# Gated product at byte 128 modulo 512 of a partition, and the last down projection in pieces of 4 contraction tiles by 512 columns

## What is computed

```python
def conv_ffn(h, w_up, conv_w, conv_b, w_down):
    u = causal_dwconv(h @ w_up, conv_w, conv_b)
    g, val = u[..., :D_FF], u[..., D_FF:]
    return (jax.nn.gelu(g, approximate=True) * val) @ w_down
...
        h = rms_norm(x, norm_ffn_pre[layer])
        f = conv_ffn(h, ffn_w_up[layer], ffn_conv_w[layer], ffn_conv_b[layer], ffn_w_down[layer])
        x = x + rms_norm(f, norm_ffn_post[layer])
```

## Time and profile before

| what | before |
|---|---|
| median of 3 runs | 1133.59 us (1133.54 to 1134.7) |
| the profiled execution's own time | 1133.48 us |
| its span in the profile | 1131.6 us |
| PE busy | 1114.8 us, 99% |
| granted clock of TensorE, mean | 0.999 |
| layer 0, down projection | about 472 to 599 us |
| layer 1, down projection with its tail | about 998 us to the end |

### The profile page before, as it was taken

The page is one execution under the profiler, slowest core; times in us unless marked ns, Lnnn a source line. Parts: engine busy times, 40 slices in busy tenths (PEclk is TensorE's granted clock), DMA queues, the critical chain, the costliest instruction groups (busy, mean ns, idle before and its releaser), DMA issues.

```text
span 1131.6 us, 16487 instructions
## 1 busy us (share of the span) xinstructions
PE 1114.8 (99%) x6564; PEld 963.5 (85%) x6564; DVE 682.2 (60%) x901; ACT 502.1 (44%) x715; POOL 68.4 (6%) x56
## 2 busy tenths in 40 slices
PE   8999999999999999999999999999999999999998
PEld 7877778998888888888899877898788888899998
DVE  5674477587776676722248677478877667652222
ACT  5556766544444343421225456554534434442221
POOL 3000000230000000001003000023000000000000
PEclk9999999999999999999999999999999999999999
DMA  7311211413243332232212624231423324222232
GB/s 222 113 59 55 66 47 61 126 42 109 76 110 98 87 111 77 99 103 93 84 66 76 181 73 152 64 86 39 111 82 103 108 78 111 86 92 96 73 103 76
DMA packets 147629, 104.50 MB, mean 92 GB/s; under 512 B 4658, under 2 KB 144626, under 8 KB 147570
## 3 DMA queue, kind: packets, MB, share of 16 engines
q1 hardware_dynamic: 147538, 103.66, 30.6%
q10 hardware_dynamic: 32, 0.01, 0.0%
HBM read 98.02 MB, written 2.10 MB: 88 GB/s over the span
## 4 chain that ended last, share of the span: by engine, by line
PE 82%; DVE 9%; issue 3%; ACT 3%; DMA 2%; SPq 1%; DVEq 0%; ACTq 0%
PE ps L1529 25%; PE ps L1531 25%; PE ps L1530 25%; PE ps L1750 2%; SPq L523 1%; DVE hx_lo L1315 1%; DVE w_lo L1025 1%; DVE ps L1305 1%; DVE x L1311 1%; PE ps L1734 1%; PE ps L1763 1%; DVE cv L1361 1%; DVE cg L1361 1%; ACT prob L980 1%; PE ps L1605 1%
## 5 line engine op out<-in xcount | busy, mean ns | idle before, releaser
L1529 PE MATMUL ps<-hx_hi,w_hi 128*128 128x512 f32 (+1 forms) x944 | 360.6, 382 | 4.4 <-DVE w_lo L1057 1.9
L1530 PE MATMUL ps<-hx_lo,w_hi 128*128 128x512 f32 (+1 forms) x944 | 354.0, 375 | 0.0
L1531 PE MATMUL ps<-hx_hi,w_lo 128*128 128x512 f32 (+1 forms) x944 | 354.0, 375 | 0.0
L1025 DVE TENSOR_TENSOR w_lo<-w_raw,w_hi 128x2048 fp32r<-128x2048 f32 (+1 forms) x87 | 194.9, 2241 | 153.8 <-ACT w_hi L647 153.7
L647 ACT ACTIVATE w_hi<-w_raw 128x2048 fp32r<-128x2048 f32 (+1 forms) x87 | 162.6, 1869 | 141.9 <-DMA w_raw<-in_ffn_w_down 112.9
L1529 PEld LDWEIGHTS ps<-hx_hi,w_hi 128*128 128x128 f32 x944 | 177.6, 188 | 40.0 <-issue 4.6
L1531 PEld LDWEIGHTS ps<-hx_hi,w_lo 128*128 128x128 f32 x944 | 177.6, 188 | 32.2
L1530 PEld LDWEIGHTS ps<-hx_lo,w_hi 128*128 128x128 f32 x944 | 177.7, 188 | 31.8 <-issue 1.7
L1529 PE MATMUL ps<-w_hi,g_hi 128*128 128x256 f32 x352 | 99.0, 281 | 0.0
L887 ACT ACTIVATE cg<-ug,vec 128x512 f32<-128x512 f32 x44 | 35.9, 816 | 141.5 <-DVE ug L1352 141.5
L1531 PE MATMUL ps<-w_hi,g_lo 128*128 128x256 f32 x352 | 98.6, 280 | 0.0
(11 more groups left out here) (238 smaller groups left out, 1669.0 us busy)
## 6 DMA issues: line engine op xcount, KB each, us to landing
w_raw<-in_ffn_w_up SPq DMA_DIRECT2D x84, 512.0 KB, 4.6
w_raw<-in_ffn_w_down SPq DMA_DIRECT2D x16, 1024.0 KB, 5.0
w_raw<-in_even_w_in SPq DMA_DIRECT2D x8, 1024.0 KB, 5.1
w_raw<-in_ffn_w_down SPq DMA_DIRECT2D x8, 768.0 KB, 4.3
w_raw<-in_odd_w_qkv SPq DMA_DIRECT2D x6, 1024.0 KB, 5.1
w_raw<-in_even_w_out SPq DMA_DIRECT2D x4, 1024.0 KB, 4.9
w_raw<-in_odd_w_o SPq DMA_DIRECT2D x3, 1024.0 KB, 5.3
rsw<-rp SPq DMA_DIRECT2D x40, 64.0 KB, 2.0
```

Source lines behind the costliest of these rows:

```text
L1025: dve.tensor_tensor(w_lo[s][:, 0:k], w_raw[s][:, 0:k], w_hi[s][:, 0:k], ALU.subtract).then_inc(w_lo_done, 1)
L1529: pe.matmul(dst, s_hi, r_hi, start=first, stop=False)
L1530: pe.matmul(dst, s_hi, r_lo, start=False, stop=False)
L1531: return pe.matmul(dst, s_lo, r_hi, start=False, stop=last)
```

## The change

It does four things. The gated product begins at the next byte that is 128 modulo 512 (160 bytes further on). The mixers' buffers begin 320 bytes behind it, at 448 modulo 512. Layer 1's down projection is cut into two halves of 512 columns with pieces of 4 contraction tiles (`WIDE_K`: five of 4 and one of 2), again 12 units; a slot of 8 tiles by 256 columns is read as 4 tiles by 512 columns. Each token tile of a half has a PSUM bank of its own, and the last two pieces of the second half run token tile by token tile. The tail has two column groups in place of four. The arithmetic per output is the same, with sums over the contraction in the same order of tiles.

```diff
+WIDE_K = [(0, 4), (4, 8), (8, 12), (12, 16), (16, 20), (20, FT)]
+WIDE_TAIL = 4
...
+    def begin_at(r):
+
+        where[0] += (r - where[0]) % 512
...
-    big0 = where[0]
+    begin_at(128)
+    g0 = where[0]
+    big0 = g0 + 320
 
     g_hi = place("g_hi", [P, FT, T], F32R)
     g_lo = place("g_lo", [P, FT, T], F32R)
+    where[0] += big0 - g0
...
+    def wide(w):
+
+        return w[:].rearrange("p (k a) b n -> p k (a b n)", a=2)
+
+    def wide_bank(half, t):
+
+        g = group_of(U_DOWN[1])
+        if half == 0:
+            return bank((group_banks(g), group_banks(g) + 1, 6, 7)[t])
+        return bank((group_banks(g + 2), group_banks(g + 2) + 1, turn_bank(0), turn_bank(1))[t])
...
+            if layer == 1:
+                for half in range(2):
+                    for c, (k0, k1) in enumerate(WIDE_K):
+                        u = U_DOWN[1] + len(WIDE_K) * half + c
+                        slot_free(u)
+                        src = w_down[k0 * P:k1 * P, T * half:T * half + T].rearrange("(k p) n -> p k n", p=P)
+                        load(u, src, wide(w_raw[slot(u)])[:, 0:k1 - k0])
+                continue
...
+        def token_squares(half, t):
+
+            if half == 0 and t == TT - 1:
+                act.wait_ge(unit_done, U_DOWN[1] + len(WIDE_K))
             else:
+                act.wait_ge(mtok_mm, (TT - 1) * half + t + 1)
+            if TT * half + t >= 2:
+                act.wait_ge(mtok_sq, TT * half + t - 1)
+            act.activation(sq[t % 2][:], wide_bank(half, t), ACT.Square, accum_out=narrow[:, t, half:half + 1]).then_inc(mtok_sq, 1)
...
+        def token_gains(half, t):
...
+            dve.wait_ge(mtok_sq, TT * half + t + 1)
+            if half == 1:
+                dve.tensor_tensor(narrow[:, t, 4:5], narrow[:, t, 0:1], narrow[:, t, 1:2], ALU.add).then_inc(tok_sum, 1)
+            cols = slice(T * half, T * half + T)
+            dve.tensor_tensor(m_tok[:, t, cols], wide_bank(half, t), last_gain[:, cols], ALU.mult).then_inc(mtok_done, 1)
...
+        def wide_part(half, t, c):
+
+            u = U_DOWN[1] + len(WIDE_K) * half + c
+            k0, k1 = WIDE_K[c]
+            r_hi, r_lo = wide(w_hi[slot(u)]), wide(w_lo[slot(u)])
             for k in range(k0, k1):
+                last = three(wide_bank(half, t), g_hi[:, k, P * t:P * t + P], g_lo[:, k, P * t:P * t + P],
+                             r_hi[:, k - k0], r_lo[:, k - k0], k == 0, k == FT - 1)
...
+            banks_free(g_end)
+            for c in range(n):
+                unit_ready(U_DOWN[1] + c)
+                pe.wait_ge(g_ready, FT + WIDE_K[c][1])
+                for t in range(TT):
+                    last = wide_part(0, t, c)
...
+                if c < 4:
+                    if c == 0:
+                        banks_free(g_end + 1)
+                    turn_x(c)
+            banks_free(g_end + 2)
             pe.wait_ge(xtok_copied, DT)
+            for c in range(WIDE_TAIL):
+                unit_ready(U_DOWN[1] + n + c)
+                for t in range(TT):
+                    last = wide_part(1, t, c)
+                last.then_inc(unit_done, 1)
+            for c in range(WIDE_TAIL, n):
+                unit_ready(U_DOWN[1] + n + c)
             for t in range(TT):
+                for c in range(WIDE_TAIL, n):
+                    last = wide_part(1, t, c)
+                last.then_inc(mtok_mm, 1)
```

More of the change, by code:

```diff
@@ L899, in ffn_up @@
             act.activation(tile_(g_hi, j), cv[:], ACT.Copy).then_inc(g_hi_done, 1)
[L901 to L906, removed]
-            else:
[L908 to L911, removed]
@@ new lines, in last_down @@
+        def last_down():
+            n = len(WIDE_K)
+            for half in range(2):
+                for c in range(n):
+                    v = U_DOWN[1] + n * half + c + 2
+                    if v < N_UNITS:
+                        k0, k1 = WIDE_K[(c + 2) % n]
+                        split_hi(v, 2 * (k1 - k0))
+                    if half == 1 and c == n - 1:
+                        act.preload_act_table_set("sqrt_and_others")
+                    if half == 0 and c < 4:
+                        for i in (2 * c, 2 * c + 1):
+                            act.wait_ge(xtok_mm, i + 1)
+                            act.activation(x_tok[:, :, P * i:P * i + P], bank(turn_bank(i)).rearrange("p (t c) -> p t c", c=P),
+                                           ACT.Copy).then_inc(xtok_copied, 1)
+                for t in range(TT):
+                    token_squares(half, t)
+                    if half == 1:
+                        act.wait_ge(tok_sum, t + 1)
+                        act.activation(std[:, t:t + 1], narrow[:, t, 4:5], ACT.Sqrt, scale=1.0 / D, bias=eps).then_inc(tok_std, 1)
@@ L930, in ffn @@
                 ffn_up(layer, j, U_UP[layer] + j)
+            if layer == 1:
+                last_down()
+                return
             for mp in range(4):
                 for c in range(3):
-                    u = U_DOWN[layer] + 3 * mp + c
+                    u = U_DOWN[0] + 3 * mp + c
                     v = u + 2
-                    if v < U_DOWN[layer] + N_DOWN:
+                    if v < U_DOWN[0] + N_DOWN:
                         k0, k1 = DOWN_K[(3 * mp + c + 2) % 3]
                         split_hi(v, k1 - k0)
[L938 to L943, removed]
-                    if c == 2 and mp < 3:
[L945 to L954, removed]
+                    if c == 2 and mp < 3:
+                        whole_squares(1, mp, u)
         out_projection(0)
@@ L1389, in last_gains, with last_down @@
             dve.wait_ge(tok_rms, t + 1)
-            dve.wait_ge(mtok_done, 6 + t + 1)
+            dve.wait_ge(mtok_done, TT + t + 1)
             dve.wait_ge(xtok_copied, DT)
             for h in range(2):
-                half = slice(h * D // 2, (h + 1) * D // 2)
-                dve.scalar_tensor_tensor(out=m_tok[:, t, half], in0=m_tok[:, t, half], scalar=rcol[:, t:t + 1],
-                                         in1=x_tok[:, t, half], op0=ALU.mult, op1=ALU.add).then_inc(out_done, 1)
+                part = slice(h * D // 2, (h + 1) * D // 2)
+                dve.scalar_tensor_tensor(out=m_tok[:, t, part], in0=m_tok[:, t, part], scalar=rcol[:, t:t + 1],
+                                         in1=x_tok[:, t, part], op0=ALU.mult, op1=ALU.add).then_inc(out_done, 1)
+        def last_down():
+            n = len(WIDE_K)
+            for half in range(2):
+                for c in range(n):
+                    v = U_DOWN[1] + n * half + c + 2
+                    if v < N_UNITS:
+                        k0, k1 = WIDE_K[(c + 2) % n]
+                        split_lo(v, 2 * (k1 - k0))
+                for t in range(TT):
+                    token_gains(half, t)
         def ffn(layer):
@@ L1935, in ffn @@
                 unit(u0 + j, hx)
-            g_up = group_of(U_DOWN[layer])
+            if layer == 1:
+                return
+            g_up = group_of(U_DOWN[0])
             for mp in range(3):
@@ L1940, in ffn @@
                 for c, (k0, k1) in enumerate(DOWN_K):
-                    u = U_DOWN[layer] + 3 * mp + c
+                    u = U_DOWN[0] + 3 * mp + c
                     unit_ready(u)
[L1943 to L1970, removed]
+                    pe.wait_ge(g_ready, k1)
@@ L1971, in last_part @@
+                    columns(u, range(k1 - k0), gg, b0, k_last=FT - 1, koff=k0, signal_first=c == 2).then_inc(unit_done, 1)
+        def wide_part(half, t, c):
+            u = U_DOWN[1] + len(WIDE_K) * half + c
+            k0, k1 = WIDE_K[c]
+            r_hi, r_lo = wide(w_hi[slot(u)]), wide(w_lo[slot(u)])
             for k in range(k0, k1):
-                r = [w[slot(u)][:, k - k0].rearrange("p b n -> p (b n)") for w in (w_hi, w_lo)]
-                last = three(last_tokens(t), g_hi[:, k, P * t:P * t + P], g_lo[:, k, P * t:P * t + P], r[0], r[1], k == 0, k == FT - 1)
@@ L2120, in _ @@
         ffn(1, 2)
-        last_unit()
+        last_down()
     es.close()
```

71 lines of the change are left out of this document (28 added, 43 removed).

## The result

The changed kernel takes 1126.30 us (median of 4 runs, 1125.82 to 1126.91), the one before 1133.57 us in the runs beside it: a ratio of 0.9936, with a 95% interval from 0.9924 to 0.9948. That is 7.3 us or 0.64% less. The forecast was 1127.0 us, between 1125.0 and 1130.5.

What follows compares the result with a forecast made beforehand. PE was taken as the bound, matmul count times pitch. −4.2 + 0.6 − 2.65 − 0.3 = −6.55 us against 1133.48 gave 1126.9, forecast as 1127.0 us for the median, range 1125.0 to 1130.5.

Steps and rivals of the forecast that it cites:

- Part 1: Layer 1's down projection: 528 matmuls of 512 columns at 226.7 ns replace 1056 of 256 at 117.3, −4.2 us.
- A fixed cost of 11 to 13 ns per matmul: Cause given for the wide pieces' gain: each matmul pays 11 to 13 ns, so two of 256 columns pay twice.
- favourable bound of 224.0: Layer 1's wide pieces: a stationary g as favourable as at 480 gives 224.0 ns per matmul, −5.6 us.
- 233.4 bound: Layer 1's wide pieces at the pitch of g moving from 480, 233.4 ns: 123.2 us, so only −0.7 us.
- What must keep up: Layer 1's down projection: unit loads, ACT's splits and DVE stay covered, 7 us to spare at worst, cost nothing.
- Part 2: The tail behind the last matmul: longer matmul, square and gain add +0.6 us, bounds 0.3 and 0.8.
- Part 3: Layer 0's down projection: 396 matmuls with g moving fall from 233.4 to 226.7 ns, −2.65 us.
- Part 4: Mixers' buffers from 480 to 448: 96 wide matmuls, half of −0.6 us taken, −0.3; stationary uses nothing.
- The place is not what makes g slow: Rival: g's pitch in layer 0 has another cause, or its new place is no better; 1130.0 us, chance 0.17.
- Wide matmuls cost 233.4: Rival: layer 1's 512-column matmuls with weights moving take 233.4 ns, not 226.7; 1130.5 us, chance 0.08.
- The fixed cost is small: Rival: a merged pair saves only 2.7 ns and g's place does nothing in layer 0; 1132.7 us, chance 0.02.
- The mixers' buffers get worse: Rival: at 448 the 864 matmuls reading the buffers cost 13.4 ns more each, +5.3 us, 1138.9 us, chance 0.02.

Runs made afterwards that it cites:

- wide_only: The kernel before with only the wide pieces, g and the mixers' buffers left at 480 modulo 512: 1133.85 us, ratio 1.000.
- place_only: The kernel before with g at 128 and the mixers' buffers at 448 modulo 512, the pieces as they were: 1132.77 us, ratio 0.9989.
- g384: The changed kernel with g at 384 in place of 128 modulo 512, the mixers' buffers still at 448: 1126.08 us, ratio 0.9939.
- g192: The changed kernel with g at 192 in place of 128 modulo 512, the mixers' buffers still at 448: 1130.4 us, ratio 0.9973.
- the last map: A matmul-only kernel in hi/lo order, varying operand offset difference, moving and stationary columns, run twice in opposite order: 226.7 ns at difference 0, 512 moving, 128 stationary columns.

## Why the prediction was right, point by point

**What bounds it.** Right: PE, by number of matmuls times pitch. Reading pitches from starts was what made the sum possible, and the 226.7 ns read from hx before was met to 0.1 ns by both down projections after.

**Part 1, −4.2 forecast, −4.72 measured.** The 226.7 ns were right; the term was mis-sized on the side of before. I read 117.3 ns from one stretch, and others of the same stage were dearer with the same operands. First and last of 61 starts in the kernel before:

```profile
1045.76 0.28 PE L1530 MATMUL ps<-w_lo,g_hi 128*128 128x256 f32 x1
...
1052.96 0.28 PE L1530 MATMUL ps<-w_lo,g_hi 128*128 128x256 f32 x1
```

7.20 / 60 = 120.0 ns. Between 1022.79 and 1042.49 it was 118.7. These pitches change at the turns of x: 117.4, 118.7, 120.0 and again 117.3 ns between one turn and the next. After the change the stage keeps 226.7 from end to end, but for the turns of x and the few steps behind them.

What this part said of causes was wrong. "A fixed cost of 11 to 13 ns per matmul, which two matmuls of 256 columns pay twice" would have given wide_only its 4 us; it gave no pitch. The favourable bound of 224.0, from a stationary g at 480, had the wrong sign: that place is cheap for 256 columns and costs 7.6 ns for 512. The 233.4 bound was about the value of the wide form without the move (234.3). I got 226.7 because I took the row with both operands at 128 as "the state after the change". That was the right row to take, but the reason given for the gain, tested alone in wide_only, was off by about 4 us: that the sum came out all the same is in part luck.

**What must keep up: right.** No step from one product to the next is above 0.31 us but at the turns of x, and those take 0.79 us from the turn's first matmul to the next product, as before. So no unit came late.

**Part 2, +0.6 forecast, +0.85 measured.** To the start of the last normalising step it is 2.01 us, before 1.54, so +0.47 of the +0.6. What is missing is on the gain: from its start to the reciprocal are 0.60 us, before 0.44, so of the 0.27 that it got longer only 0.16 are on the path. Another 0.38 comes from there to the end, 4.27 us against 3.89, and was not forecast. It lies behind equal steps and equal stores: the last store has landed 0.76 us before the end of the span, before the change 0.41. In between, SP's last branch (1123.04) and its closing drain (1123.51) are 0.46 us apart, where they were 0.17, and the drain takes 0.07 us in place of 0.01. The wide pieces alone have it (0.47), the place alone hasn't (0.17). So it belongs to the end of SP's program, which the wide pieces rewrote; why it is longer there is not shown.

**Part 3, −2.65 forecast, −2.66 measured**, by the very step. It was tested alone (place_only, 123.07 us) with the same result.

**Part 4, −0.3 forecast.** The stretches with the mixers lost 0.58 and 0.69 us against before, but the wide pieces alone, with the same buffers as before, differ from it by +0.45 and −0.61. The steps are steadier. From one start to the next of the same pair, the wide ones over y, ya and yb take 20.4 us in all, where they took 20.7: the forecast 0.3. The narrow ones, which I took as unchanged, take 54.6, where they took 55.8, since they went from 120 to 118 ns or less; the `w_x` ones 20.6, where they took 20.8. The place alone and g384 have the same within 0.3 us. So the term was mis-sized: 1.5 to 1.8 us of PE's steps in place of 0.3.

**The rivals.** "The place is not what makes g slow" is out by layer 0's 226.7, and so is its variant, that 640 modulo 2048 is no better. "Wide matmuls cost 233.4" is out here and about true one move away, in wide_only (234.3) and g192 (233.3): it was the most instructive of the rivals and had 0.08. "The fixed cost is small" was nearer to the cause than to the time: merging by itself saved next to nothing, and 512-column steps are cheap only in the right place. The Trainium skill's 2.5 ns per matmul ("TensorE: Matmul & The Clock Gate", Back-to-back issue gap) was not seen at any place: the least over the columns' own time was 6.6 ns (113.3 at 256) and 13.4 ns (226.7 at 512). That section gives the 2.5 ns for an isolated matmul, which the prediction left out; for a stream of weight loads and matmuls it gives about 131 ns at 512 columns, and this trace does not agree with that either. "The mixers' buffers get worse" is out: at 448 their steps got cheaper.

## What to carry to other kernels

Where PE is the bound, read the pitch from starts, stretch by stretch, and for each pair of operands write down where both lie. Two parts of a change that seem separate may be worth something only together: a part measured alone (0.0% and 0.1% here, 0.64% together) can be thrown away by mistake. Choose the width of the moving operand and the places together. Here, with float32r and 128 stationary columns, 512 moving columns were cheapest with both operands at the same offset modulo 256 (226.7 ns). For 256 columns that was among the dearest (120.0), and so was a difference of 96; differences of 64 and 192 gave 113.3 or 117.9.

## What the hardware showed that I had not expected

- Two fp32r operands' offsets in the partition act on each other with a period of 256 bytes: 226.7 to 234.3 ns for 512 columns, 113.3 to 120.0 for 256. The same offset is the cheapest for the first and among the dearest for the second. The Trainium skill's statement in "TensorE: Matmul & The Clock Gate", Step-by-step, that weight loads take no read bandwidth from the moving operand, is not refuted by this, since the mechanism is open, but the two are not independent in time.
- Within one stretch a pitch is constant, as far as the trace resolves it, but for the first few steps behind a turn of x; after an interruption the same operands may run at another pitch (117.3, 118.7 or 120.0 ns in layer 1's down projection before the change; 113.3 or 117.9 ns for the same series in the two turns of the last map).
- With 128 columns moving, a step is 111.7 ns with 128 stationary columns and 60.0 with 64 or with 32, at every difference tried. So at 128 and 128 the stationary operand's size sets the pace, and place does not count.
